# Differential attention: scores of two query blocks as one run, and the norm's column by sixteen small products

## The reference, cut to what matters

```python
logits = einsum('bhmqs', q_block, k) * scale + bias      # m = 2 maps
logits = where(allowed, logits, NEG_INF)                 # chunks of 64, causal
p = softmax(logits, axis=-1)
attn = p[:, :, 0] - lam * p[:, :, 1]
o = einsum('bhqs,bshe->bqhe', attn, v)
```

## Time and profile before

| | |
|---|---|
| median of three runs | 2545.89 us |
| the profiled execution | 2545.68 us |
| its span, first to last instruction | 2543.9 us |
| TensorE busy | 2484.5 us, 98% |
| VectorE busy | 1472.0 us, 58% |
| ScalarE busy | 1165.0 us, 46% |
| mean granted TensorE clock | 0.997 |

### The profile page before, as it was taken

The page is one execution under the profiler, slowest core; times in us unless marked ns, Lnnn a source line. Parts: engine busy times, 40 slices in busy tenths (PEclk is TensorE's granted clock), DMA queues, the critical chain, the costliest instruction groups (busy, mean ns, idle before and its releaser), DMA issues.

```text
span 2543.9 us, 36073 instructions
## 1 busy us (share of the span) xinstructions
PE 2484.5 (98%) x14504; PEld 2017.5 (79%) x14504; DVE 1472.0 (58%) x2374; ACT 1165.0 (46%) x2099; POOL 160.2 (6%) x156
## 2 busy tenths in 40 slices
PE   9999999999999999999989999999999999999998
PEld 6888778888776688888867888888877877788886
DVE  6665554433656564344378898786666556543343
ACT  5354352322456644233256666665455444432232
POOL 2110110000200010000101111111000010100001
PEclk9999999999999999999999999999999999999999
DMA  5222134544322223333322222222322233233322
GB/s 154 76 60 76 58 101 115 127 110 117 102 79 77 66 83 94 97 99 96 95 91 75 67 59 75 69 82 75 95 63 62 89 120 108 75 108 100 92 99 75
DMA packets 197093, 226.50 MB, mean 89 GB/s; under 512 B 7552, under 2 KB 132768, under 8 KB 196672
## 3 DMA queue, kind: packets, MB, share of 16 engines
q1 hardware_dynamic: 196928, 224.21, 30.0%
HBM read 214.22 MB, written 9.44 MB: 88 GB/s over the span
## 4 chain that ended last, share of the span: by engine, by line
PE 81%; DVE 10%; ACT 6%; issue 3%; DMA 0%; POOL 0%; DVEq 0%; SPq 0%; ACTq 0%; POOLq 0%
PE bank L1982 22%; PE bank L1984 22%; PE bank L1983 22%; DVE CV L2716 2%; PE bank L1988 1%; PE bank L1989 1%; PE bank L1990 1%; DVE wlo L2480 1%; PE bank L2001 1%; ACT whi L2259 1%; PE bank L2191 1%; DVE h L2514 1%; PE bank L2199 1%; ACT XAh L2268 1%; PE bank L2212 1%
## 5 line engine op out<-in xcount | busy, mean ns | idle before, releaser
L2480 DVE TENSOR_TENSOR wlo<-raw,whi 128x1024 fp32r<-128x1024 f32 x389 | 489.6, 1264 | 627.3 <-ACT whi L2259 625.0
L2259 ACT ACTIVATE whi<-raw 128x1024 fp32r<-128x1024 f32 x389 | 408.9, 1058 | 582.2 <-PE bank L1984 569.2
L1982 PE MATMUL bank<-XAh,whi 128*128 128x512 f32 x1552 | 616.0, 397 | 11.4 <-issue 4.4
L1983 PE MATMUL bank<-XAl,whi 128*128 128x512 f32 x1552 | 602.1, 388 | 0.0
L1984 PE MATMUL bank<-XAh,wlo 128*128 128x512 f32 x1552 | 602.1, 388 | 0.0
L1982 PEld LDWEIGHTS bank<-XAh,whi 128*128 128x128 f32 x1552 | 291.7, 188 | 90.7 <-issue 22.4
L1984 PEld LDWEIGHTS bank<-XAh,wlo 128*128 128x128 f32 x1552 | 291.9, 188 | 61.1
L1983 PEld LDWEIGHTS bank<-XAl,whi 128*128 128x128 f32 x1552 | 292.1, 188 | 57.5 <-issue 1.0
L1982 PE MATMUL bank<-XBh,whi 128*128 128x512 f32 (+1 forms) x840 | 331.2, 394 | 1.8 <-DVE XBl L2486 1.7
L1984 PE MATMUL bank<-XBh,wlo 128*128 128x512 f32 (+1 forms) x840 | 323.9, 386 | 0.0
L1983 PE MATMUL bank<-XBl,whi 128*128 128x512 f32 (+1 forms) x840 | 323.8, 386 | 0.0
(11 more groups left out here) (346 smaller groups left out, 3299.8 us busy)
## 6 DMA issues: line engine op xcount, KB each, us to landing
raw<-in_w_in SPq DMA_DIRECT2D x77, 512.0 KB, 3.9
raw<-in_up SPq DMA_DIRECT2D x64, 512.0 KB, 3.7
raw<-in_down SPq DMA_DIRECT2D x64, 512.0 KB, 3.7
raw<-in_a_w_in SPq DMA_DIRECT2D x32, 512.0 KB, 4.1
raw<-in_w_up SPq DMA_DIRECT2D x32, 512.0 KB, 3.7
raw<-in_w_down SPq DMA_DIRECT2D x32, 512.0 KB, 3.6
raw<-in_w_kv SPq DMA_DIRECT2D x16, 512.0 KB, 3.7
raw<-in_w_ssd_branch SPq DMA_DIRECT2D x16, 512.0 KB, 3.5
```

What stands on the lines that cost most here:

```text
L1982: pe.matmul(out, wh[:, w, c], xh[:, x, r], start=st, stop=False)
L1983: pe.matmul(out, wh[:, w, c], xl[:, x, r], start=False, stop=False)
L2259: act.activation(s.hi, s.raw, ACT.Copy).then_inc(s.whi[0], 1)
L2480: dve.tensor_tensor(s.lo, s.raw, s.hi.bitcast(F32), ALU.subtract).then_inc(s.wlo[0], 1)
```

## The change

A generator `score(hd, js)` now takes two blocks, first (1, 2), then (0, 3) of each head. It starts when four probability buffers and four banks are free, places both `df_mm` in a row, then both `df_exp`; after one piece both `df_mix`; after two pieces, for each block, `df_tr` and `df_at`. The extra piece that block 0 waited for is gone. The step `rcol` makes sixteen products with 32 output partitions each in place of four with 128.

```diff
-        def score(hd, j):
+        def score(hd, js):
             while qtok[hd] is None or ktok[hd] is None:
                 yield WAIT
-            if j == 0:
-                yield from p.spaced(1)
-            while (started[p.pieces] and not p.hurry) or hd not in tokT or not Pt.room(2) or not ring_all.room(3) or (...):
+            while (started[p.pieces] and not p.hurry) or hd not in tokT or not Pt.room(4) or not ring_all.room(4) or (...):
                 yield WAIT
...
+            of = []
+            for j in js:
+                w = (j + 1) * P
+                bs = [ring_all.take(), ring_all.take()]
+                s1 = add("df_mm", Q=QT, K=KT, hd=hd, j=j, w=w, banks=bs, ...)
+                of.append((j, w, bs, s1.mm))
+            rows = []
+            for j, w, bs, mm in of:
+                pr = [Pt.take(), Pt.take()]
+                cs = [stt[:, hd * 8 + j * 2 + mp, :] for mp in range(2)]
+                s2 = add("df_exp", banks=bs, pr=pr, cs=cs, T=Ts, ...)
+                for b, v in zip(bs, s2.top):
+                    b.free(v)
+                rows.append((j, w, pr, cs, s2.exp))
...
             yield
             yield from p.spaced(1, begun)
+            mixed = []
+            for j, w, pr, cs, exp in rows:
+                s3 = add("df_mix", pr=pr, cs=cs, w=w, exp=exp, ...)
+                pr[1].free(s3.mix)
+                mixed.append(s3.mix)
+                yield
             yield from p.spaced(2, begun)
+            for (j, w, pr, cs, exp), mix in zip(rows, mixed):
+                while not ring_all.room(1):
+                    yield WAIT
+                b = ring_all.take()
+                s4 = add("df_tr", src=pr[0], j=j, bank=b, mix=mix, tr=sig("df.tr"))
+                pr[0].free(s4.tr)
+                s5 = add("df_at", bank=b, j=j, at=H["at"], o=tri(j), tr=s4.tr, ...)
...
         def heads():
             for hd in range(8):
-                for j in range(4):
-                    yield score(hd, j)
+                yield score(hd, (1, 2))
+                yield score(hd, (0, 3))
                 yield values(hd)
...
             for i in range(4):
-                m = pe.matmul(s.bank.t[:, 2 * i:2 * i + 1], s.r.t[0:1, i * P:(i + 1) * P], K.ones[0:1, 0:1], start=True, stop=True)
+                for b in range(4):
+                    m = pe.matmul(s.bank.t[b * 32:b * 32 + 32, 2 * i:2 * i + 1], s.r.t[0:1, i * P + b * 32:i * P + b * 32 + 32], K.ones[0:1, 0:1], start=True, stop=True)
```

More of the change, by code:

```diff
@@ L1168, in tri @@
             return j * (j + 1) // 2 * P
-        def score(hd, j):
+        def score(hd, js):
             while qtok[hd] is None or ktok[hd] is None:
                 yield WAIT
-            if j == 0:
-                yield from p.spaced(1)
-            while (started[p.pieces] and not p.hurry) or hd not in tokT or not Pt.room(2) or not ring_all.room(3) or (hd not in hs and not ATs.room(1)):
+            while (started[p.pieces] and not p.hurry) or hd not in tokT or not Pt.room(4) or not ring_all.room(4) or (hd not in hs and not ATs.room(1)):
                 yield WAIT
@@ L1180, in score @@
             Ts, Tk = tokT[hd]
[L1181 to L1184, removed]
             started[p.pieces] += 1
             begun = p.pieces
[L1187 to L1191, removed]
+            of = []
+            for j in js:
+                w = (j + 1) * P
+                bs = [ring_all.take(), ring_all.take()]
+                s1 = add("df_mm", Q=QT, K=KT, hd=hd, j=j, w=w, banks=bs, q_ready=qtok[hd], k_ready=ktok[hd], mm=[sig("df.mm"), sig("df.mm")])
+                of.append((j, w, bs, s1.mm))
[3 more added lines that the diff above has]
+                cs = [stt[:, hd * 8 + j * 2 + mp, :] for mp in range(2)]
+                s2 = add("df_exp", banks=bs, pr=pr, cs=cs, T=Ts, T_ready=Tk, T_ends=T_ends, w=w, j=j, mm=mm, scope_free=end,
+                         top=[sig("df.top"), sig("df.top")], neg=[sig("df.neg"), sig("df.neg")], exp=[sig("df.exp"), sig("df.exp")])
+                for b, v in zip(bs, s2.top):
+                    b.free(v)
+                rows.append((j, w, pr, cs, s2.exp))
             if j == 3:
@@ L1198, in score @@
             yield from p.spaced(1, begun)
-            s3 = add("df_mix", pr=pr, cs=cs, w=w, exp=s2.exp, inv=sig("df.inv"), scaled=sig("df.scaled"), mix=sig("df.mix"))
-            pr[1].free(s3.mix)
-            yield
-            yield from p.spaced(2, begun)
[L1203 to L1211, removed]
+            mixed = []
+            for j, w, pr, cs, exp in rows:
+                s3 = add("df_mix", pr=pr, cs=cs, w=w, exp=exp, inv=sig("df.inv"), scaled=sig("df.scaled"), mix=sig("df.mix"))
+                pr[1].free(s3.mix)
+                mixed.append(s3.mix)
+                yield
+            yield from p.spaced(2, begun)
+            for (j, w, pr, cs, exp), mix in zip(rows, mixed):
[4 more added lines that the diff above has]
+                pr[0].free(s4.tr)
+                s5 = add("df_at", bank=b, j=j, at=H["at"], o=tri(j), tr=s4.tr, scope_free=end, at_done=sig("df.at"))
+                b.free(s5.at_done)
+                H["ev"].append(s5.at_done)
+                yield
         def values(hd):
```

## The result

| | before | after |
|---|---|---|
| median, 5 runs each on the same chip | 2545.89 us | 2564.20 us (2563.51 to 2565.39) |
| ratio, 95% interval | | 1.0072 [1.0061, 1.0082] |
| profiled execution, its span | 2545.68, 2543.9 us | 2565.39, 2563.6 us |
| first scores to the end of the last ones product beside heads | 718.59 to 889.08, 170.5 us | 717.13 to 908.84, 191.7 us |

The kernel is 18.3 us slower. The direction was forecast, the size was not: 2556.7 us stood in the prediction, and 2564.2 lies 1.2 us beyond the upper end of its range. The last line of the table locates the whole difference: the attention stage is 21.2 us longer where 12.8 were expected (11.1 and a clock fall of 1.7), the stage starts 1.5 us earlier, and what follows it takes the same 1654.8 us in both.

The account below looks back on a forecast made before the run. TensorE, busy 98%, bounds the kernel, with the chain scores, exponentials, mix nearly a second bound. 2545.7 + 11.1 (stage, 4.9 saving inside) - 1.8 (columns) + 1.7 (clock) = 2556.7 us; own range 2552 to 2561, 8 in 10: 2543 to 2563.

Parts of the forecast that it names:

- Work of TensorE: Attention stage: 16 merged score runs save 3.4 us, joined projection pieces 1.5; 4.9 us taken, bounds 0 and 6.8.
- pieces that join: Attention stage: about 11 slots without scores, transposes or values join two projection pieces unbroken, 0.14 us each, 1.5 us saved.
- Column products: Three places before projection products: sixteen small products replacing four save 1.8 us in all, bounds 0 and 2.9.
- Second halves: From scores of blocks 0 and 3 to the next head's: 8.6 us, or 10.7 if that head is even.
- First halves: From a head's scores of blocks 1 and 2 to those of 0 and 3: 10.9 us, set by TensorE.
- T' = T + 10.9: On TensorE, a head's pair (0, 3) starts at T', 10.9 us after its pair (1, 2) starts at T.
- After slot 24: From 118.8 us into the stage: one 12.0 us chain, three pairs at 8.6, finally 23.8 us without waits.
- The clock: TensorE's granted clock falls once among the waits before slots 8, 16 and 24: 1.7 us, bounds 0 and 5.1.
- A: Attention-stage chain keeps up, only savings left: 2539.0 us; decides at 7.3 us from T' to first mix; chance 0.15.
- B: Attention stage: only the three query waits stay, 6.3 us; 2545.3 us, no change; chance 0.15.
- C: Clock falls at all three waits for query tiles, chain as summed: 2560.1 us; chance 0.15.
- D: Attention-stage pairs placed less often than every second slot, four lost slots: 2568 us; chance 0.08.

Follow-up runs that it names:

- the later split: Changed kernel, pairs still in even slots, with each attention-stage weight split placed one piece later, behind both mixes: 2547.57 us, ratio 1.0006.
- the pairs alone: Changed kernel with the four old products in `rcol`, so only the merged pairs of blocks differ from the kernel before: 2564.24 us, ratio 1.0075.
- the products in the waits: Changed kernel with one or two extra width-512 products ahead of TensorE's waits that preceded clock falls: 2562.29 us, ratio 1.0066.
- later values: Changed kernel with each head's values' product one piece later, the ones product falling in a slot without scores: 2559.85 us, ratio 1.0053.
- later ones product: Kernel with the split behind the mixes, plus heads 0 to 3's ones product one piece later and its bank handed out last: 2564.11 us, ratio 1.0071.
- wide block first: Kernel with the split behind the mixes, with the second pair of blocks taken as (3, 0) instead of (0, 3): 2550.14 us, ratio 1.0016.
- the column products alone: Kernel before with only the sixteen small products in place of four, no pairs: 2544.41 us, ratio 0.9994.

## Why the prediction was wrong in size

**Work of TensorE.** The merged runs save what was said: 0.32 and 0.96 us instead of 0.42 and 1.06 for widths 128 and 512, 0.2 us per pair, 3.4 in all. The further 1.5 us for pieces that join isn't shown. Taking the listed waits out of the stage gives 165.6 us before (170.5 less 4.9) and 162.1 us with the later split (172.8 less 6.5 and four times 1.06), 3.5 us apart. This is an estimate: short waits aren't listed, and the two falls of the clock with the later split are still in it.

**Column products.** 1.8 us forecast, 1.5 found by the medians. 32 records took 0.35 us, 11 ns each, so the row was the right guide. The Trainium skill ("TensorE: Matmul & The Clock Gate", Wait — 56ns, not 53.3ns?) has no start closer than about 25 ns; the trace of this form disagrees.

**Second halves.** 8.6 us forecast where an odd head comes next and 10.7 where an even one does; 8.71 and 10.73 measured. Part of the way there was another, and in that part the hit was luck: the 1.06 us of the bank is in neither sum, and it doesn't show, because the pair's end is set by the chain on VectorE and ScalarE.

**First halves, the step that failed.** "T' = T + 10.9. The first mix is ready by then; TensorE sets this half." Measured 12.66, 12.27, 12.65 and 12.26 us for heads 1 to 4: 6.2 us over. In heads 1 and 3 the values' product waits 1.3 us for the copy behind four exponentials, behind a key tile's scaling that itself stands behind late mixes; the rest is short waits, about 0.15 us ahead of the transposes at 734.77 and 0.3 behind them. I costed this half by TensorE's list alone, and did not follow the chain through it as I did in the second half. In heads 2 and 4 the excess is a clock fall each, 1.25 us, as the kernel of the pairs alone and the products in the waits show. So of the 6.2 us about 2.5 are the clock, and 3.7 are waits that the sum had not.

**After slot 24.** The slots from 24 to 26 took 9.1 us against 12.0 (842.83 to 851.97), those from 26 to 28 12.5 against 8.6 (851.97 to 864.50): 1.1 us over together. The delay by the four low parts was costed for the pair they stand in and came in the next one. They take VectorE 2.5 us from 851.47 and hold up the second mix, a transposes' copy stands behind that mix's scaling on ScalarE, and at 855.00 TensorE waits 1.68 us for the bank of that copy, at the low clock. From the last transposes to the end it took 25.7 us against 23.8. A fall near 884 us is 1.6 of that; "nothing to wait for" also missed 0.58 us of the values' product at 897.24, a wait that the kernel before has too, at 876.99.

**The clock.** One fall at 1.7 us was counted; there were six. "Each fall is 1.7 us" was near (1.25 us behind a head's scores, 1.6 among projection products), "one of three" too few: two of the three query waits were followed by one, and three more waits beside heads that the sum had not looked at. Two falls in the first halves and the one near 884 us are 4.1 us; what the others cost isn't shown. The Trainium skill's warning of idle gaps between bursts ("TensorE: Matmul & The Clock Gate", Why this matters for your kernels) holds here as a warning: the waits that ended at 756.74, 801.10, 831.88, 851.61 and 882.75 us were each followed by a fall. The one of 1.56 us at 842.83 was not, and neither was the one of 1.95 us at 757.57 in the kernel of the pairs alone.

**Sum.** First halves 6.2, slots 24 to 28 1.1, last stretch 1.9, small ones 0.9: 10.1 us over the 181.6 of the prediction, less the 1.7 counted apart for the clock, is 8.4. The stage starts 1.5 us earlier and nothing is gained behind it, 0.3 less than counted for the column products. Together 8.7, which is 2565.4 of the profiled execution less 2556.7.

**Rivals.** A (2539, the chain keeps up) made it depend on the time from T' to the end of the first mix, 7.3 us; the changed kernel has 8.4 (746.01 to 754.40), as forecast. With the split behind the mixes it is 5.3 (744.15 to 749.46), and the kernel stays at 2547.6: waits for copies, banks and one query tile remain, so A's condition wasn't enough. B's 6.3 us for the three query waits measured 5.5, but it was not alone. C had three falls at the query waits, and two came, with others elsewhere. D did not happen: every pair stands in its even slot.

**What stays open.** Whether the bank's wait of 1.06 us in each of four second halves can be had back without a new one: three ways of moving it (later values, later ones product, wide block first) took it away or shortened it, and each brought another wait. None of the kernels is faster than the one before beyond its interval; the column products alone come nearest, 0.9994 [0.9985, 1.0003].

## What to carry to other kernels

When an engine's queue is a fixed order, cost a step that is split over two engines (high part on one, low part on the other) by what stands behind its second half in the queue, not by its own duration: here it put 3.1 us between an exponential and the mix behind it, and moving it by one piece was worth 16.6 us in one kernel and cost 21 in another. When a chain over several engines is nearly as long as the engine that bounds the kernel, follow it through every part of the cycle, above all the part in which it seems to have time. And before merging steps to save fixed costs, compare what is saved (3.4 us) with what the larger step makes late.

## What the hardware showed that was not expected

- The 32 records of sixteen products with 32 output partitions and one column took 0.35 us, 11 ns each on average; the 8 records of four products with 128 output partitions took 0.98 us, 122 ns each. So the wider form costs more per record by far, though both have one column. Whether that is the weight load before each product, whose record is 0.19 us long in the wide form and 0.11 in the narrow one, wasn't tested.
- A stretch of 3.4 us at 1.2 GHz cost 1.25 us behind a head's scores (12.27 us against 11.03 in the kernel of the pairs alone, whose trace has no fall there) and 1.6 us among projection products (25.7 against 24.1), where half of 3.4 us would be 1.7. Why it is less behind the scores wasn't shown.
- The same wait of 1.95 us was followed by a fall in one execution (756.74) and not in another (757.57).
- With TensorE shown busy for 5.00 of 5.00 us the granted clock was 0.66 (757 to 762 us), and with 4.93 of 5.00 it was 1.00 in the kernel with extra products: the busy share can't tell a fall, since records are drawn longer.
